# Seven products of block sums in place of eight block products in 14 panels of an MLP's first matrix

## The reference

```python
merged = jax.nn.sigmoid(gate_a) * (a @ w_oa) + jax.nn.sigmoid(gate_b) * (b @ w_ob)
x = x + merged @ w_o
h2 = _rmsnorm(x, g_ffn)
x = x + jnp.square(jax.nn.relu(h2 @ w_ff1)) @ w_ff2      # 1024 -> 4096 -> 1024
gate = jax.nn.sigmoid(_rmsnorm(x, g_ple) @ w_ple_gate)
x = x + gate * (pe @ w_ple_proj)
```

## Time and profile before

| | us |
|---|---|
| median of three runs | 1081.11 |
| lowest and highest | 1078.65, 1081.2 |
| span of the profiled execution | 1076.3 |
| median less span | 4.8 |
| TensorE busy | 1043.8 (97% of the span) |
| VectorE busy | 690.3 (64%) |
| ScalarE busy | 484.1 (45%) |
| GpSimd busy | 242.7 (23%) |

### The profile page before, as it was taken

The page is one execution under the profiler, slowest core; times in us unless marked ns, Lnnn a source line. Parts: engine busy times, 40 slices in busy tenths (PEclk is TensorE's granted clock), DMA queues, the critical chain, the costliest instruction groups (busy, mean ns, idle before and its releaser), DMA issues.

```text
span 1076.3 us, 21532 instructions
## 1 busy us (share of the span) xinstructions
PE 1043.8 (97%) x8507; PEld 1030.8 (96%) x8508; DVE 690.3 (64%) x881; ACT 484.1 (45%) x1181; POOL 242.7 (23%) x374
## 2 busy tenths in 40 slices
PE   8999999999987999999999999999999999999996
PEld 8999999999987998999999999999999999999996
DVE  5579888988887778999583354344434443445552
ACT  6772888569634664352264543123312321333331
POOL 2441334014210014949101210010001000102300
PEclk9999999999998999999999999999999999999999
DMA  6557565776797564777732345555555555555512
GB/s 199 197 174 233 189 199 177 258 223 209 218 264 234 177 199 146 220 202 209 244 117 77 106 144 196 166 186 191 194 168 184 191 197 174 182 188 166 165 41 83
DMA packets 131090, 196.20 MB, mean 182 GB/s; under 512 B 32208, under 2 KB 108272, under 8 KB 129216
## 3 DMA queue, kind: packets, MB, share of 16 engines
q1 hardware_dynamic: 105808, 122.46, 35.9%
q0 software_dynamic: 10304, 63.28, 18.6%
q10 hardware_dynamic: 14896, 9.34, 2.9%
HBM read 186.07 MB, written 62.00 MB: 230 GB/s over the span
## 4 chain that ended last, share of the span: by engine, by line
PE 67%; DVE 13%; ACT 6%; issue 5%; DMA 4%; SPq 4%; ACTq 1%; POOL 0%; DVEq 0%; POOLq 0%
PE gm L1112 53%; PE gm L1088 3%; PE gm L1089 3%; PE gm L1090 3%; DMA w_raw<-in_w_in 2%; DVE w_lo L1391 2%; ACT prob L953 2%; DVE kv L1553 2%; DVE kv L1512 1%; DVE acc L1559 1%; SPq L587 1%; ACT sq L663 1%; SPq L539 1%; ACT w_hi L644 1%; ACTq L968 1%
## 5 line engine op out<-in xcount | busy, mean ns | idle before, releaser
L1112 PE MATMUL gm<-h_hi,w_hi 128*128 128x272 f32 x1088 | 227.8, 291 | 0.3 <-issue 0.3
L1112 PE MATMUL gm<-h_hi,w_lo 128*128 128x272 f32 x1088 | 225.1, 288 | 0.0
L1112 PE MATMUL gm<-h_lo,w_hi 128*128 128x272 f32 x1088 | 224.3, 288 | 0.0
L644 ACT CAST w_hi<-w_raw 128x1024 fp32r<-128x1024 f32 x150 | 150.5, 1044 | 157.9 <-PE gm L1112 116.5
L1391 DVE TENSOR_TENSOR w_lo<-w_raw,w_hi 128x1024 fp32r<-128x1024 f32 x150 | 178.2, 1227 | 40.2 <-ACT w_hi L644 38.0
L1088 PE MATMUL gm<-w_hi,h_hi 128*128 128x256 f32 x640 | 187.3, 293 | 4.6 <-issue 4.4
L1089 PE MATMUL gm<-w_hi,h_lo 128*128 128x256 f32 x640 | 181.1, 283 | 0.0
L1090 PE MATMUL gm<-w_lo,h_hi 128*128 128x256 f32 x640 | 180.3, 282 | 0.0
L1112 PEld LDWEIGHTS gm<-h_hi,w_hi 128*128 128x128 f32 x1088 | 170.5, 188 | 1.1 <-issue 0.5
L1112 PEld LDWEIGHTS gm<-h_lo,w_hi 128*128 128x128 f32 x1088 | 171.0, 189 | 0.0
L1112 PEld LDWEIGHTS gm<-h_hi,w_lo 128*128 128x128 f32 x1088 | 169.9, 189 | 0.0
(11 more groups left out here) (263 smaller groups left out, 1531.3 us busy)
## 6 DMA issues: line engine op xcount, KB each, us to landing
w_raw<-in_w_ff SPq DMA_DIRECT2D x64, 512.0 KB, 5.1
out_kvs<-in_cache_kv_w POOLq DMA_DIRECT2D x64, 510.0 KB, 4.3
w_raw<-in_w_in SPq DMA_DIRECT2D x60, 512.0 KB, 6.4
kv<-in_cache_kv_w SPq DMA_DIRECT2D x128, 128.0 KB
kv<-in_cache_kv_w SPq DMA_DIRECT2D x64, 256.0 KB
out_kvs<-in_cache_kv_w POOLq DMA_DIRECT2D x32, 508.0 KB, 4.8
kv<-in_cache_kv_w POOLq DMA_DIRECT2D x128, 64.0 KB, 3.5
w_raw<-in_w_o SPq DMA_DIRECT2D x8, 512.0 KB, 4.8
```

The source lines that it names most:

```text
L644: nc.scalar.copy(w_hi[:, r, hh * 1024:(hh + 1) * 1024], w_raw[:, hh]).then_inc(w_hi_done, 1)
L1112: last = nc.tensor.matmul(gm[:, 2 * b2 + half, 0:HALF], w, x[:, k0 + k, half * HALF:(half + 1) * HALF], start=first, stop=end)
```

## The change

In a panel of `w_ff1` the product of a 1024x256 matrix with a 1024x544 input can be seen as a 2x2 arrangement of blocks times a 2x2 arrangement: rows and columns of the panel in halves (512 rows, 128 columns), columns of the input in halves of 272. That is eight block products of 12 matmuls each (4 row blocks × 3 part products). In 14 of the 16 panels of `w_ff1` (all but the first two of group 0, `seven(p)`) seven products of sums of blocks take their place, named p1, p2, p5, p6, p4, p3, p7 in the order in which they run.

- TensorE (`seven_products`): 84 matmuls of 128x272 in such a panel. A product goes into one PSUM bank, and p6 and p7 go on in the bank of p1, p3 in that of p5.
- The input's sums t1 to t4 are made once, in the first two panels of group 0: ScalarE scales the residual (`gain_x`, eight of 128x544), VectorE makes four sums (`combine`, 128x1088), ScalarE four high parts, VectorE four low parts.
- The weights' sums are made for each panel: VectorE adds blocks in place in the raw buffers (`add_blocks`, four of 128x4x128), and three halves and one block (`one_hi`, `one_lo`, 128x512) are split in place of two halves.
- Behind the products ScalarE copies four half results out of PSUM (`part`, 128x272), VectorE adds the bank pair and the copies (`add_parts`), and squares with the relu in one instruction (`square_parts`); ScalarE casts the high part, VectorE subtracts for the low part. There is no relu or square on ScalarE in such a panel.
- There are two raw buffers (`w_raw`, `w_more`) that take turns from panel 3 of group 0 on. `w_more` lies in space that is free when panel 2 of group 0 begins.
- The MLP's PSUM banks are now four pairs (`gm` twice, `psT`, `psSO`), which `psS` and `psO` were made one tensor for.
- The loops over the groups are written out on every engine.

The core of the diff (blank lines dropped; the first `hidden_panel` is ScalarE's; of VectorE's the start is shown, the order below gives the rest):

```diff
+def seven(p):
+    j, q = divmod(p - P_FF, FF_PANELS)
+    return P_FF <= p < P_PG and q < 4 and (j > 0 or q >= 2)
...
+PRODUCTS = ("p1", "p2", "p5", "p6", "p4", "p3", "p7")
...
+            def load_panel(p):
+                q = raw_before(p)
+                j = (p - P_FF) // FF_PANELS if P_FF <= p < P_PG else None
                 for hh in range(2):
-                    if not (isinstance(pp, int) and pp == 0):
-                        sp.wait_ge(w_lo_done, 2 * (pp - 1) + hh + 1)
-                    nk = 1024 // (256 if j is not None or p >= P_PG else COLS.get(PANELS[p][0], 256))
-                    sp.dma_start(w_raw[:, hh].rearrange("p (k n) -> p k n", k=nk), wview(p, hh, j)).then_inc(w_landed[hh], 16)
+                    if q is not None:
+                        sp.wait_ge(w_lo_done, SPLITS[q] + (4 - hh if seven(q) else hh + 1))
+                    if raw_set(p) and raw_loads(p) == 1:
+                        sp.wait_ge(unit_ready, PANEL_START[ff_panel(0, 2)])
+                    nk = 1024 // (256 if p >= P_FF else COLS.get(PANELS[p][0], 256))
+                    dst = raw(p, hh) if p >= P_FF else w_raw[:, hh].rearrange("p (k n) -> p k n", k=nk)
+                    sp.dma_start(dst, wview((p - P_FF) % FF_PANELS if j is not None else p, hh, j)).then_inc(w_landed[raw_set(p)][hh], 16)
...
+            def part(p, n):
+                bank, dst = ((1, sq[:, 0, 0:HALF]), (0, sq[:, 1, HALF:NT]), (1, sq[:, 0, HALF:NT]), (1, sq[:, 1, 0:HALF]))[n]
+                act.wait_ge(unit_ready, READY[p, ("p1", "p5", "p6", "p7")[n]])
+                x = SEVENS.index(p)
+                if x:
+                    act.wait_ge(unit_out, U_FF + 2 * (SEVENS[x - 1] - P_FF) + 1 + n % 2)
+                else:
+                    act.wait_ge(ss_done, KD)
+                u = U_FF + 2 * (p - P_FF)
+                src = banks(u + 1)[:, 1, 0:HALF] if bank else banks(u)[:, 1, 0:HALF]
+                nc.scalar.copy(dst, src).then_inc(part_out, 1)
...
+            def hidden_panel(p):
+                j, q = divmod(p - P_FF, FF_PANELS)
+                new, after = seven(p), seven(p + 1)
+                if seven(p - 1):
+                    part(p - 1, 3)
+                if new and not seven(p - 1):
+                    sums_hi(p, 0, 2)
+                if after:
+                    one_hi(p + 1)
+                else:
+                    raw_hi(p + 1, 0)
+                if new:
+                    part(p, 0)
+                if after:
+                    raw_hi(p + 1, 1)
+                elif not new:
+                    raw_hi(p + 1, 1)
+                if seven(p - 1):
+                    squares_hi(p - 1, 0)
+                    squares_hi(p - 1, 1)
+                if new:
+                    part(p, 1)
+                    part(p, 2)
+                    if not after:
+                        raw_hi(p + 1, 1)
+                    else:
+                        sums_hi(p + 1, 1, 1)
+                        sums_hi(p + 1, 0, 2)
+                    return
...
+                if after:
+                    sums_hi(p + 1, 1, 1)
...
+            def product(p, name, bank, w, x, start):
+                for k in range(4):
+                    for wx, xx in ((0, 0), (0, 1), (1, 0)):
+                        last = nc.tensor.matmul(bank[:, 0:HALF], w[wx][:, k], x[xx][:, k], start=start and k == 0 and wx == xx,
+                                                stop=k == 3 and wx == 1, skip_group_check=True)
+                last.then_inc(unit_ready, 1)
+            def seven_products(p):
+                n, u, s = SEVENS.index(p), U_FF + 2 * (p - P_FF), PAIRS[p]
+                (A, C), (Dd, B) = (banks(u)[:, 0], banks(u)[:, 1]), (banks(u + 1)[:, 0], banks(u + 1)[:, 1])
+                one = [x[:, n % 2].rearrange("p (k n) -> p k n", k=4) for x in (w_one_hi, w_one_lo)]
+                bd, yu, wv = [[[block_of(w_pair(x, s + y), m) for x in (w_hi, w_lo)] for m in range(2)] for y in range(3)]
+                first, second = slice(0, HALF), slice(HALF, NT)
+                x11, x21, x22 = [[x[:, k:k + 4, cols] for x in (h_hi, h_lo)] for k, cols in ((0, first), (4, first), (4, second))]
+                t1, t2, t3, t4 = [[xc_hi[x], xc_lo[x]] for x in range(4)]
+                pe.wait_ge(w_lo_done, SPLITS[p] + 1)
+                pair_free(u + 1)
+                product(p, "p1", B, one, x11, True)
+                pe.wait_ge(w_lo_done, SPLITS[p] + 2)
+                pair_free(u)
+                product(p, "p2", A, bd[0], x21, True)
+                pe.wait_ge(w_lo_done, SPLITS[p] + 3)
+                if n == 0:
+                    pe.wait_ge(xc_lo_done, 4)
+                product(p, "p5", C, yu[1], t1, True)
+                pe.wait_ge(w_lo_done, SPLITS[p] + 4)
+                pe.wait_ge(part_out, 4 * n + 1)
+                product(p, "p6", B, wv[0], t2, False)
+                product(p, "p4", Dd, bd[1], t4, True)
+                pe.wait_ge(part_out, 4 * n + 2)
+                product(p, "p3", C, yu[0], x22, False)
+                pe.wait_ge(part_out, 4 * n + 3)
+                product(p, "p7", B, wv[1], t3, False)
...
+            def add_blocks(p, n):
+                top, low = [[raw(p, hh)[:, :, 128 * m:128 * m + 128] for m in range(2)] for hh in range(2)]
+                out, other = ((low[1], top[1]), (top[1], top[0]), (top[0], low[1]), (low[0], top[0]))[n]
+                if n == 0:
+                    dve.wait_ge(w_lo_done, SPLITS[p] + 2)
+                else:
+                    dve.wait_ge(w_summed, 4 * SEVENS.index(p) + n)
+                vec.tensor_tensor(out, out, other, ALU.add).then_inc(w_summed, 1)
+            def add_parts(p, m):
+                u = U_FF + 2 * (p - P_FF) + m
+                dve.wait_ge(unit_ready, READY[p, ("p3", "p7")[m]])
+                dve.wait_ge(part_out, 4 * SEVENS.index(p) + 3 + m)
+                j, uu = divmod(2 * (p - P_FF) + m, FF_UNITS)
+                if uu >= 2:
+                    dve.wait_ge(hid_hi, j * KD + uu - 1)
+                    dve.wait_ge(hid_lo, j * KD + uu - 1)
+                else:
+                    dve.wait_ge(z_used, j * FF_UNITS + zc(U_FF) - 1)
+                vec.tensor_tensor(z[:, m].rearrange("p (n c) -> p n c", n=2), banks(u)[:, :, 0:HALF],
+                                  sq[:, m].rearrange("p (n c) -> p n c", n=2), ALU.add).then_inc(unit_out, 1)
...
+            def hidden_panel(p):
+                j, q = divmod(p - P_FF, FF_PANELS)
+                new, after = seven(p), seven(p + 1)
+                if seven(p - 1):
+                    add_parts(p - 1, 0)
+                if new and not seven(p - 1):
+                    pair_lo(p, 0, 2)
...
-            with pool.Fori(0, NFF - 1) as j:
-                window_parts(j)
-            window_parts(NFF - 1, final=True)
+            for j in range(NFF):
+                window_parts(j, j == NFF - 1)
```

More of the change, by code:

```diff
@@ L607, in _ @@
                     sp.dma_start(pns[:], t["p_sample"]).then_inc(p_in, 16)
[L608 to L617, removed]
+            for p in range(P_FF, P_PG + 4):
+                load_panel(p)
             sp.wait_ge(cache_copied, 16 * (64 + 32 + 16))
@@ L1032, in _ @@
+            for p in range(P_FF, P_PG):
+                hidden_panel(p)
             for i in range(4):
                 if i < 3:
-                    split_hi(P_PG + i + 1, (P_PG + i + 1) % 2, U_PG + 2 * i)
+                    raw_hi(P_PG + i + 1, 0)
+                    raw_hi(P_PG + i + 1, 1)
                 for sub in range(2):
@@ L1111, in block_unit @@
                         for half in range(2):
-                            last = nc.tensor.matmul(gm[:, 2 * b2 + half, 0:HALF], w, x[:, k0 + k, half * HALF:(half + 1) * HALF],
+                            last = nc.tensor.matmul(pair[:, half, 0:HALF], w, x[:, k0 + k, half * HALF:(half + 1) * HALF],
                                                     start=first, stop=end)
@@ new lines, in hidden_panel @@
+            def hidden_panel(p):
+                j, q = divmod(p - P_FF, FF_PANELS)
+                new, after = seven(p), seven(p + 1)
[3 more added lines that the diff above has]
+                    pair_lo(p, 0, 2)
+                if after:
+                    one_lo(p + 1)
+                else:
+                    pair_lo(p + 1, 0, 0)
+                if not new and not after:
+                    pair_lo(p + 1, 1, 1)
+                if seven(p - 1):
+                    add_parts(p - 1, 1)
+                if after:
+                    pair_lo(p + 1, 1, 0)
+                if seven(p - 1):
+                    square_parts(p - 1, 0)
+                if after:
+                    add_blocks(p + 1, 0)
+                if seven(p - 1):
+                    square_parts(p - 1, 1)
+                if after:
+                    add_blocks(p + 1, 1)
+                if seven(p - 1):
+                    squares_lo(p - 1, 0)
+                if after:
+                    add_blocks(p + 1, 2)
+                if seven(p - 1):
```

(40 more changed lines are left out.)

296 lines of the change are left out of this document (204 added, 92 removed).

## The result

The changed kernel takes 1084.13 us in the median of 14 runs (1079.32 to 1087.95), the kernel before 1078.72 in as many (1076.27 to 1081.2). The ratio is 1.0043, with a 95% interval of 1.003 to 1.0055: slower by 0.43%, or 5.4 us between the medians. The forecast was 1076.5 us, a gain.

The account below looks back on a forecast made before the run. TensorE was taken to bound the kernel: 21.05 us saved, less 3 × 3.7 for groups 1 to 3 and 5.3 for group 0, left 4.6 off 1081.1, giving 1076.5 us; range 1067 to 1083.

Parts of the forecast that it names:

- What bounds it, and the saving: MLP: TensorE sets the end; 14 panels with 12 fewer matmuls each at 0.1253 us save 21.05 us.
- more than 0.1253 apart: New panels: sign that the forecast is wrong, if matmuls staying in one PSUM bank are spaced wider than 0.1253 us.
- VectorE's panel: New panels: VectorE needs 11.5 us, including waiting for ScalarE's cast, for each 10.52 us of TensorE.
- rival B: New panels: VectorE's steps take full length plus 0.04 us each, 13.2 us with the cast; 1092.8 us, chance 0.09.
- The waits of groups 1 and 2: TensorE loses 0.3 us in panel 1, 0.9 in panel 2, 2.5 in the first `w_ff2` unit: 3.7 a group.
- Group 0: First group: two new panels save 3.0 us, waits in panels 2, 3 and first `w_ff2` unit cost 5.3: 2.3 slower.
- The first failed step: Weight loads into raw buffers: a later load has 9 us against at most 6.3 needed, so it is hidden.
- The second failed step: TensorE's clock in the MLP: no slowdown after the waits was counted in the sum.
- rival C: MLP: four longest TensorE waits each lower its clock, costing 3 us apiece; 1088.5 us, chance 0.05.
- Rival D: Order as forecast, but load, hand-overs and added waits take 2 to 4 us more; 1080 us, chance 0.14.
- the hand-over of "some 0.28" us: MLP: a result is taken up some 0.28 us after TensorE starts the next unit.
- The base: Whole kernel before: profiled span of 1076.3 us plus 4.8 us around it, giving the median of 1081.1 us.

Follow-up runs that it names:

- the experiment: The changed kernel with panel 5 of group 3 loaded into the second raw buffer, not the one panel 4 still occupies: 1079.98 us, ratio 1.0004.

## Why the prediction was wrong

- **What bounds it, and the saving:** right. Matmuls that follow one another in one bank keep their pace: panel 3 of group 1, without waits, takes 10.57 us, 0.1258 a matmul, where 10.52 and 0.1253 were forecast. The sign "more than 0.1253 apart" is met by so little that it is worth 0.7 us in all.
- **VectorE's panel:** right. 11.5 us were forecast; from one pair of last low parts to the next it is 11.75 in the timeline:

```profile
735.80 2.36 DVE L1623 TENSOR_TENSOR w_lo<-w_more,w_hi 128x1024 fp32r<-128x1024 f32 x2 [1.11 <-ACT w_hi L740]
...
747.55 2.36 DVE L1623 TENSOR_TENSOR w_lo<-w_raw,w_hi 128x1024 fp32r<-128x1024 f32 x2 [1.11 <-ACT w_hi L740]
```

Steps that don't need their neighbour's result start 0.60 to 0.64 us apart, as taken, though each lasts 0.68 to 0.72:

```profile
742.03 0.69 DVE L1641 TENSOR_TENSOR w_raw<-w_raw 128x512 f32<-128x512 f32 x1
742.64 0.72 DVE L1660 SCALAR_TENSOR_TENSOR z<-z 128x544 f32<-128x544 f32 x1
743.27 0.68 DVE L1641 TENSOR_TENSOR w_raw<-w_raw 128x512 f32<-128x512 f32 x1
743.87 0.72 DVE L1668 TENSOR_TENSOR x_lo<-z,x_hi 128x544 fp32r<-128x544 f32 x1
```

So rival B, full lengths, is out: panel 2 takes 11.72 and not 13.2. The Trainium skill's sentence in VectorE: DVE Perf Modes, "The DRAIN you can't avoid", that the next operation does not start until the pipe is empty, doesn't hold for these neighbours. The same section adds that an operation that is not held starts earlier. The prediction left that out, and these rows agree with it.
- **The waits of groups 1 and 2:** right in place and size: panel 1 loses 0.3 us (10.83 less 10.57), TensorE stands 0.9 before p3 of panel 2, and 2.09 in unit 8.
- **Group 0:** right in sum: 2.8 us slower than before, 2.3 forecast. The places differ. The load cost less in panel 2 (12.5 us instead of 13.1), because the cast of the block and p6 came in time; ScalarE stood for the other half instead, and that late start of VectorE made panel 3 take 11.96, not 10.7. The starts of panels 2 and 3 and of unit 8:

```profile
651.13 0.29 PE L1536 MATMUL psSO<-h_hi,w_one_hi 128*128 128x272 f32 x1
...
663.65 0.29 PE L1536 MATMUL gm<-h_hi,w_one_hi 128*128 128x272 f32 x1
...
675.61 0.42 PE L1293 MATMUL psT<-x_hi,w_hi 128*128 128x272 f32 x2
```

- **The first failed step** is "A later load starts when the low parts of the panel two before are done ... hidden", in the part on other edits. It holds while the two buffers take turns. The text ahead of the prediction says that they do so from panel 3 of group 0 on; in group 3 they don't from panel 5 on, and the forecast had not followed the buffer rule to that group. The price was put at nothing and is 3.7 us of waiting, 4.2 in time by the experiment.
- **The second failed step** is the clock, which the sum put at nothing and rival C got 0.05 for. Its mechanism was right and it came true. Its price of 3 us for each of four waits was too high: 1.6, 1.6 and 1.9 in three groups, 5.1 in all. That is more than the load cost. The reason given against it, that only a gap about twice as long had lowered the clock, came from one pair of rows of one execution. The trace of the kernel before has a wait between the two, of 2.34 us, and it left the clock at 1.00. The same wait, behind the same work ahead of the MLP, lowered it in the profile of the changed kernel. First the kernel before, then the changed one, each with the row of the wait's end and a row of busy time (columns as in rows 2):

```profile
428.72 0.49 PE L1112 MATMUL gm<-x_hi,w_hi 128*128 128x272 f32 x2 [2.34 <-DVE w_lo L1391]
426.00:430.00 4.00, 1.66 (x14) 1.47 (x13) 3.96 (x5) 1.42 (x3) 0.00 (x0) 1.00 0.31 89
...
428.18 0.49 PE L1293 MATMUL gm<-x_hi,w_hi 128*128 128x272 f32 x2 [2.33 <-DVE w_lo L1616]
430.00:432.00 2.00, 2.00 (x11) 2.00 (x11) 1.97 (x3) 0.00 (x0) 1.24 (x3) 0.50 0.75 247
```

It lowered the clock in the profiles of all seven experiments too, that of the kernel before with written-out loops among them. So one execution that kept its clock says little against the rival.
- **Rival D**, a load, hand-overs and waits that take 2 to 4 us more, has the kind and size of the first failed step but not its place. With the load late and the clock kept up, the time was 1079.0: gain and loss cancel, as D says.
- **Two readings:** the hand-over of "some 0.28" us is 0.38 by the first of its two pairs of rows, and rows 1 don't show that two thirds of the span were written out. Neither moves the sum: the written-out loops cost nothing that can be told.
- **The base:** I took 4.8 us around the profiled span; the changed kernel's profiled run has 1.8 (1083.74 less 1081.9), and the kernel before measured again is 1078.7, not 1081.1. The absolute forecast was 2.4 us high by this.

The sum again, by the unit starts of the two profiles: group 0 is 2.8 us slower (2.3 forecast), groups 1 and 2 are 0.6 faster each (2.3), group 3 is 3.4 slower (2.3 faster forecast). That is 5.0 slower instead of 4.6 faster, so the forecast is off by 9.6. The clock takes 5.1 of that and the late load 3.7; 0.8 are left, 0.5 of them in group 0. By the medians, 4.6 less 4.2 less 5.1 gives 4.7 slower, and 5.4 are measured. Behind the last unit the changed kernel's profile is 0.6 us longer; 0.4 of that are its last transposes, four of which take 0.91 us instead of 0.49 at a granted clock of 0.50.

What remains open is why the same wait of 2.09 us left the clock at 1.00 in group 0. The waits of 2.33 us above say that the length of the wait and the work around it don't settle it: with both the same, one execution in nine kept its clock.

## What to carry to other kernels

Saving a tenth of TensorE's work in a stage is worth what the followers' order allows: here the same instructions in another order on two engines turned a version that was 0.43% slower into one that is 1.3% faster. Follow each engine's order, step by step, through the boundary between two kinds of stages and through the last turn of every rule on buffers, as closely as through the steady part. A wait of TensorE that other work can't fill should be priced with the low clock behind it, at least as a bound, and a rival on the clock should be judged from several executions.

## What the runs showed of the hardware that was not expected

In the profile of the changed kernel a wait of 2.1 us was followed by the lower clock level in groups 1 and 2 and not in group 0, and one of 5.8 us in group 3; with the load moved all three of groups 1 to 3 were 2.1 us and were followed by it. A wait of 2.33 us ahead of the MLP was followed by it in eight of nine profiled executions. The gap of 1.5 us in the earlier trace rows had left it alone. In the MLP the low level cost 1.6 to 1.9 us each time, and filling the waits with matmuls whose results are thrown away was worth 5.1 us.
